# The order of gate scatters and row gathers on one DMA queue, in the experts stage of a hybrid decoder layer

## What is computed

```
q = (xb @ w_query).reshape(tn, PEER_HEADS, 2, PK_HALF)
s = einsum('thkd,hknd->thkn', q, sub_keys);  top_s, top_i = top_k(s, 16)
...
best_s, best_j = top_k(cand_s, 16)             # 16 experts for each of 8 heads
gates = softmax(best_s)
act = gelu(einsum('thkd,td->thk', expert_u[experts], xb))
out = einsum('thk,thkd->td', gates * act, expert_v[experts])
```

## Time and profile before

| | |
|---|---|
| median of 3 runs | 5192.61 us (5158.98 to 5197.61) |
| span of the profiled execution | 5087.9 us |
| TensorE matmul busy | 4732.6 us (93%) |
| DVE busy | 3153.2 us (62%) |
| POOL busy | 1567.5 us (31%) |
| moved by DMA | 1377.05 MB, mean 271 GB/s |
| experts stage, from its first gather to the end | 2826 to 5088 us |
| scatters issued | 3349.5 to 4155.4 us |

### The profile page before, as it was taken

How to read it: one execution, slowest core, us unless ns; L and a number is a source line. 1 busy time by engine, 2 the same in 40 slices (tenths; PEclk the granted TensorE clock), 3 DMA queues, 4 the chain that set the end, 5 groups by cost and what they waited for, 6 DMA issues and landing times. The chain is left out here.

```text
span 5087.9 us, 68117 instructions
## 1 busy us (share of the span) xinstructions
PE 4732.6 (93%) x27237; PEld 3798.3 (75%) x27237; DVE 3153.2 (62%) x4952; ACT 1249.9 (25%) x1562; POOL 1567.5 (31%) x1385
## 2 busy tenths in 40 slices
PE   8999999999978888899999899999999938899997
PEld 7999999999976555898789555555555526677776
DVE  2323443333436666433457588889778876888987
ACT  2212323233322222322354000000000003334433
POOL 0110000000014444000000222256655564788850
PEclk9999999999988899999999999999999969999998
DMA  5533333233339998524556899999999999999995
GB/s 192 200 141 115 99 107 108 94 111 102 102 110 344 352 355 301 185 106 173 174 206 224 324 421 418 405 410 394 386 395 397 395 387 355 411 408 407 409 407 199
DMA packets 346087, 1377.05 MB, mean 271 GB/s; under 512 B 85396, under 2 KB 128692, under 8 KB 220200
## 3 DMA queue, kind: packets, MB, share of 16 engines
q0 software_dynamic: 138464, 727.19, 35.7%
q1 hardware_dynamic: 176536, 613.34, 32.8%
q10 hardware_dynamic: 30768, 32.11, 1.9%
HBM read 1277.05 MB, written 111.66 MB: 273 GB/s over the span
## 5 line engine op out<-in xcount | busy, mean ns | idle before, releaser
L2262 PE MATMUL i_ps<-f_xT,i_ut 128*128 128x384 f32 x4096 | 1326.6, 487 | 83.6 <-DMA i_ut<-in_u_tiles 83.6
L2262 PEld LDWEIGHTS i_ps<-f_xT,i_ut 128*128 128x128 f32 x4096 | 779.9, 191 | 628.4 <-issue 89.1
L300 PE MATMUL a_acc<-a_xh,a_wh 128*128 128x288 f32 x3104 | 673.2, 299 | 19.1 <-DVE a_xl L526 13.7
L300 PE MATMUL a_acc<-a_xh,a_wl 128*128 128x288 f32 x3104 | 666.4, 296 | 0.0
L300 PE MATMUL a_acc<-a_xl,a_wh 128*128 128x288 f32 x3104 | 665.6, 296 | 0.0
L2674 POOL DMA_INDIRECT i_row<-in_expert_v,f_ei x320 | 481.6, 1505 | 245.2 <-DVE i_sum L2511 97.2
L2511 DVE SCALAR_TENSOR_TENSOR i_ps<-i_row,i_cf,i_ps 128x2048 f32<-128x2048 f32 x190 | 447.5, 2355 | 136.1 <-DMA i_row<-in_expert_v,f_ei 127.0
L300 PEld LDWEIGHTS a_acc<-a_xh,a_wh 128*128 128x128 f32 x3104 | 500.4, 189 | 30.6 <-issue 28.4
L300 PEld LDWEIGHTS a_acc<-a_xl,a_wh 128*128 128x128 f32 x3104 | 501.6, 189 | 0.0
L300 PEld LDWEIGHTS a_acc<-a_xh,a_wl 128*128 128x128 f32 x3104 | 501.4, 189 | 0.0
L2502 DVE CUSTOM_DVE_ANT_0 i_row<-i_row,i_ps 128x2048 f32<-128x2048 f32 x192 | 430.4, 2284 | 98.2 <-DMA i_row<-in_expert_u,f_ei 95.8
(11 more groups left out here) (372 smaller groups left out, 7342.7 us busy)
## 6 DMA issues: line engine op xcount, KB each, us to landing
i_ut<-in_u_tiles SPq DMA_DIRECT2D x128, 1024.0 KB, 9.6
i_ut<-in_expert_v SPq DMA_DIRECT2D x128, 1024.0 KB, 13.1
a_w<-in_w_in SPq DMA_DIRECT2D x97, 1024.0 KB, 5.0
f_w<-in_w_out SPq DMA_DIRECT2D x32, 1024.0 KB, 4.9
f_w<-in_w_query SPq DMA_DIRECT2D x32, 1024.0 KB, 5.2
tmp_Ha<-i_ho ACTq DMA_DIRECT2D x128, 192.0 KB, 9.1
tmp_uT<-a_out POOLq DMA_DIRECT2D x65, 288.0 KB, 2.3
tmp_Wd<-in_zeros SPq DMA_DIRECT2D x16, 1024.0 KB, 7.3
```

What stands on the lines that cost most here:

```text
L300: last = nc.tensor.matmul(acc[:, 2 * slot + h, 0:HALF], weights[:, wslot, k * P:(k + 1) * P], x[:, k, h * HALF:(h + 1) * HALF], start=(k = ...
L2262: last = nc.tensor.matmul(p_h[:, e % 2, 0:ND], ut[:, e % RU, k * P:(k + 1) * P], xT[:, k, :], start=(k == 0), stop=(k == KT - 1))
```

## The change

It touches one function, `scatters_by`. The sixteen scatters of a head are issued in four groups of four, one group behind each of the head's first four gathers. The head's other gathers (seven of 11 for the first dense tile, twelve of 16 for the second) follow with none between them. Number and order of gathers and of scatters, all waits and all other engines' programs stay as they are. The last four scatters stand behind gather 347, where the last one stood behind gather 359.

```diff
                 def scatters_by(m):
-                    return 0 if m < 144 else PICKS * (m - 143) // 88 if m < 232 else min(2 * PICKS, PICKS + m - 231)
+                    if m < 144:
+                        return 0
+                    first, every = (144, 11) if m < 232 else (232, 16)
+                    h, at = divmod(m - first, every)
+                    return min(2 * PICKS, (0 if m < 232 else PICKS) + TOPK * h + min(TOPK, 4 * (at + 1)))
```

## The result

The changed kernel takes 5216.42 us (median of 8 runs, 5210.02 to 5223.59), the kernel before 5187.47 us on the same chip. The ratio is 1.0057, 95% interval 1.0038 to 1.0075: slower by about 30 us, where 35 us less were forecast.

What follows compares the result with a forecast made beforehand. It took DMA engines, DVE and POOL as close together, with the end of DVE's V additions setting the time. Terms 30 + 0 + 5 = 35 us off the 5192.6 us median gave 5158 us, range 5120 to 5200.

Steps and rivals of the forecast that it cites:

- The burst: POOL's issue at a head's start: four gathers with their scatters, 6.4 us apart, 25.7 us in all.
- The wait: POOL's waits for earlier scatters to land at head ends: 160.6 us in sum, to fall under 20.
- Bandwidth in the V part above 400 GB/s: Bytes moved while V gathers run among scatters, 3566 to 4257 us: from 392 to above 400 GB/s.
- DVE's waits for rows, 127 to 95: DVE's idle time for V rows from 3566 to 4257 us: 127.0 us, to fall near 95.
- TensorE's stall of 78.07 us to 33: TensorE's idle time before its last six U tiles, behind the last scatter: 78.07 us, to fall to about 33.
- The picks' wait shorter than 30.91 us: POOL's next work, the picks, waiting for TensorE's last tiles: below 30.91 us, starting at 4216 us.
- V products at 4236 us: TensorE's V products, behind the last V addition: start near 4236 us instead of 4266.
- the gain, 30 us: V part, 3566 to 4257 us: 33.9 us of lost DMA share less 3.9 where DVE is full, so 30.
- The 5 us for the overlap of the picks: Stretch from 4257 to 4300 us: picks starting 14 us earlier against the adds' end, worth 5 us.
- The starved ring: Rival: bursts bring too few gathers and the row ring runs empty; 60 us slower, 5253 us, chance 0.08.
- Nothing moves: Rival: DMA engines are the bound and issue order adds no bandwidth; 8.5 us less, 5184 us, chance 0.15.
- Theory A: Experiments' theory: the changed order leaves TensorE, DVE and ACT short of instructions in the experts stage; changed kernel 1.005 to 1.008.

Runs made afterwards that it cites:

- before_again: The kernel before, unchanged, run and traced a second time; ratio 0.9993 to the kernel before.
- paced_before: The kernel before with one small POOL iota behind each scatter to slow issue; 5155.91 us, ratio 0.9977 to the kernel before.
- paced_after: The changed kernel with one small POOL iota behind each scatter to slow issue; 5138.48 us, ratio 0.9945 to the kernel before.
- after: The changed kernel in its first trace; 5216.42 us, ratio 1.0057 to the kernel before.
- after_again: The changed kernel, unchanged, run and traced a second time; ratio 1.0068 to the kernel before.
- group2: The changed kernel with two scatters behind each of a head's first eight gathers instead of four behind four; ratio 1.0055 to the kernel before.
- half_scatter: The changed kernel with each scatter cut to the first 64 of its 128 tokens; ratio 1.0135 to the kernel before.

## Why the prediction was wrong

**Step by step.** *The burst:* 25.7 us forecast, 4 x 6.38 = 25.5 measured. *The wait:* under 20 us forecast, 0 in every kernel with the changed order and its one wait a head. *Bandwidth in the V part above 400 GB/s:* 376. *DVE's waits for rows, 127 to 95:* 56.5, but most likely for another reason, since a DVE that crawls asks for fewer rows. *TensorE's stall of 78.07 us to 33:* 4.8, again because TensorE came late by itself. *The picks' wait shorter than 30.91 us:* 15.8. *V products at 4236 us, or 1407 after the first U product:* 1505.

**The step that failed** is the opening of "The change part by part": the change removes and adds nothing, and scatters and gathers are issued as before, "at 1.28 us each", so its issue costs what it cost. That priced a longer unpaused run of DMAs at nothing, and it costs DVE 42 us. The second term that failed is the gain, 30 us for rows that come sooner: against before_again DVE waits 16.8 us more for them, and with the crawl held down 9.2 us less (below). Nothing in the rows of before shows the first price: POOL's runs there are as long (15 of 23 to 41 DMAs, 29 to 53 us) and no engine crawls. But a sign was there. The span was 104.7 us below the median, and I wrote that "the change touches none of it". Such a gap doesn't lie around the span: every later profiled execution took only 1.6 to 2.2 us longer than its span, and no timed run of the kernel before, on any chip, took less than 5146 us. The two traces of before lie 109 us apart, 37 us of them in this very stage (V products at 1437 and 1474 us) and 75 us ahead of it (first U product at 2828.9 and 2904.3 us). The stage priced, with 160.6 us of waits and 127.0 us of missing rows, isn't the stage as it usually runs, with 69.6 and 45.0.

**What was right, and its size.** Where the crawl is small, the forecast's mechanism shows. From paced_before to paced_after the waits for scatters go from 124.0 us to 0, DVE's waits for rows from 113.6 to 104.4, and TensorE's wait for U tiles from 93.2 to 23.6 (78 to 33 was forecast). From the last U dot to the first V product it takes 699 us instead of 719 by the traces, the U part 735 instead of 732, and what follows the V products 820 instead of 819: 20 - 3 - 1 = 16 us, against 17.4 measured. But of those 20 us only 9.2 are rows that come sooner, which is the term that I had put at 30; another 9.6 are less issue idle (27.3 and 17.7 us). So a lost DMA share is not yet time that can be had: in the first trace 34 to 44 us were lost by share and bytes, and where POOL's 124.0 us of waits were filled, DVE got its rows 9 us sooner. The 5 us for the overlap of the picks brought nothing.

**The rivals.** The starved ring, slower at 5253 us, was the only one on the right side and had 0.08. Its mechanism accounts for 17 of the 59 us that DVE lost. The rest is a mechanism on no list. "Nothing moves" was wrong too. That an order of issue adds no bandwidth was my assumption; no row showed it. Here the byte rate did follow from how POOL issued (376 and 401 GB/s in the V parts of after and paced_after), by way of the engines that use the rows.

**What stays open.** What in the chip holds the other engines isn't known: the runs told the DMA rate from size, direction and a busy POOL, and no more. Nor is it known why the first execution of before was free of it, with POOL issuing 0.78 DMAs a us, 41 of them in a row, so the rate alone doesn't decide it; and whether an execution with no profile of its own crawls as much is shown only by the times, which fit.

## What to carry to other kernels

Look at "issue" idle times of all engines in a trace: when they come on several at once, in short steps, while one queue issues indirect DMAs back to back, suspect the issue rate and try a pause: a small one between them (here 0.24 us on each scatter, 0.78 down to 0.68 DMAs a us) was worth more here than any order. A change that takes waits out of an issuing engine can also take out the pauses that others lived on, as here (DVE's issue idle time 91.8 us in before_again, 133.8 in after_again); price the longer run too. And a profiled execution that lies 2% under the median of the runs may be of another regime: take a second trace and compare the stages before pricing any of them.

## What the runs showed of the hardware

- In the traces of after and before_again, where POOL issues indirect DMAs every 1.28 us, TensorE, DVE and ACT slow down without a wait that the trace shows: ACT after 12 of them or fewer (an eviction due 15.2 us into a run came late, before_again), TensorE after some 20 (25.0 to 28.4 us into a run, after). The first trace of before is an exception: there 41 in a row did nothing. In after TensorE falls to one matmul of 0.48 to 0.80 us every 2.1 to 2.8 us, and its granted clock goes from 1.00 (3684 to 3703 us) to a mean of 0.53 (3703 to 3738 us), 0.50 from 3705.2 us on; before it fell, at 3705.1 us, TensorE had been idle since 3701.9 us but for one matmul of 0.48 us. DVE stands still for up to 9.3 us and then does several short instructions in a row; ACT starts an eviction up to 39 us late.
- For TensorE it ends 2.5 to 6 us after POOL stops (after). At 0.68 DMAs a us DVE's idle time on issue is nearly gone (17.7 us of 1434, paced_after); at 0.78 it is 92 us in before_again and 134 to 154 us in after, after_again and group2.
- Theory A took the engines to be short of instructions. The page of after counts 218 packets, 3.57 MB, on a DMA queue of the kind "instruction" (q8, 16.4 KB each). One of them lies inside the crawl of 3703 to 3738 us; it took 0.93 us, where the mean of all 218 is 1.04 us. The crawl goes on over 13 matmuls in 35 us, which I don't take for the look of one late packet; that is an argument, not a test. No run here tried that path.
- The same scatters with 64 instead of 128 elements take POOL 1.2 instead of 1.28 us each (half_scatter and after): half the elements took 0.08 us off an issue.
